# A two-layer hybrid trunk on one core: index scores and later projections interleaved, wide rows counted by ScalarE, experts' second halves one expert later

## The reference

```python
def dsa_mixer(q, k, v, q_idx, k_idx, w_idx, positions, n_sel):   # n_sel = 256
    ...
        rel = jax.nn.relu(jnp.einsum('bqjd,bkd->bqjk', qi_blk, k_idx).astype(F32))   # 8 index heads of 64
        score = jnp.einsum('bqjk,bqj->bqk', rel, wi_blk)
        score = jnp.where((k_pos[None, :] <= q_pos[:, None])[None], score, -jnp.inf)
        _, sel = lax.top_k(score, n_sel)
```

```python
    def expert_block(args):
        xb, e = args
        return (jax.nn.silu(xb @ w_gate[e]) * (xb @ w_up[e])) @ w_down[e]
```

## Time and profile before

| | |
|---|---|
| median of 3 runs | 3084.16 us (3083.2 to 3084.48) |
| the profiled execution | 3082.44 us, of which the span of its instructions is 3080.7 us |
| granted clock of PE, mean | 0.906 of 2.4 GHz |
| PE busy | 2610.5 us (85%) |
| DVE, ACT, POOL busy | 1381.8, 766.0, 375.7 us |
| moved by DMA | 370.42 MB |

### The profile page before, as it was taken

One profiled execution on the slowest core, in us unless ns is written; L12 is line 12 of the kernel. 1 busy time (PEld: TensorE's weight loads), 2 busy tenths in 40 slices (PEclk: granted clock), 3 DMA queues, 4 the chain that ended last, 5 costly groups with the idle time before them and its releaser, 6 DMA issues.

```text
span 3080.7 us, 30243 instructions
## 1 busy us (share of the span) xinstructions
PE 2610.5 (85%) x10356; PEld 1470.3 (48%) x10374; DVE 1381.8 (45%) x3164; ACT 766.0 (25%) x1630; POOL 375.7 (12%) x372
## 2 busy tenths in 40 slices
PE   5979768978999879999579897598889995999994
PEld 2564324545664534444335643245556644444442
DVE  4351498985551321111342516799755414111115
ACT  2121243144450111111112214321545311111112
POOL 0000177100000000000200003750000000000002
PEclk8989958999999889999789897599999997999996
DMA  5100001120000479999311000013010005799974
GB/s 212 39 28 23 28 1 40 41 84 32 11 1 16 165 263 336 333 332 336 144 57 52 1 23 28 0 50 113 2 42 1 10 28 212 285 336 336 335 260 177
DMA packets 105453, 370.42 MB, mean 120 GB/s; under 512 B 20754, under 2 KB 39912, under 8 KB 80744
## 3 DMA queue, kind: packets, MB, share of 16 engines
q1 hardware_dynamic: 91500, 318.41, 29.2%
q0 software_dynamic: 13824, 50.34, 4.3%
HBM read 304.42 MB, written 64.30 MB: 120 GB/s over the span
## 4 chain that ended last, share of the span: by engine, by line
PE 62%; DVE 22%; POOL 5%; issue 5%; ACT 4%; DMA 1%; DVEq 1%; ACTq 0%; SPq 0%; POOLq 0%
PE bank L1017 14%; PE bank L719 9%; PE bank L1034 8%; PE bank L965 7%; DVE group_arena L1671 7%; PE bank L722 6%; PE bank L753 5%; PE bank L683 5%; POOL group_arena L620 4%; PE bank L782 3%; DVE residual L1967 1%; PE bank L1024 1%; PE bank L978 1%; DVE softmax_stats L1512 1%; DVE group_arena L1445 1%
## 5 line engine op out<-in xcount | busy, mean ns | idle before, releaser
L719 PE MATMUL bank<-w_ring,normed_cols 128*128 128x260 f32 (+4 forms) x1280 | 419.0, 490 | 9.8 <-ACTq L1254 8.6
L719 PEld LDWEIGHTS bank<-w_ring,normed_cols 128*128 128x128 f32 x1280 | 245.9, 193 | 183.0 <-issue 158.3
L683 PE MATMUL bank<-ident,group_arena 128*128 128x128 f32 (+1 forms) x1200 | 198.0, 305 | 129.2 <-DVE group_arena L1445 59.8
L722 PE MATMUL bank<-normed_cols,w_ring 128*128 128x512 f32 x640 | 281.5, 601 | 15.5 <-DMA w_ring<-in_w_in 14.3
L640 POOL DMA_INDIRECT group_arena<-h_rows,group_arena x64 | 60.3, 942 | 1631.8 <-DVEq L1927 948.5
L1034 PE MATMUL bank<-heads_cols,group_arena 128*128 128x512 f32 x512 | 236.5, 604 | 7.8 <-DVE group_arena L1937 4.2
L914 PE MATMUL bank<-group_arena 64*128 64x512 f32 (+3 forms) x320 | 159.8, 814 | 95.7 <-ACTq L1254 93.8
L683 PEld LDWEIGHTS bank<-ident,group_arena 128*128 128x128 f32 (+1 forms) x1200 | 148.0, 154 | 189.1 <-issue 94.8
L1017 PE MATMUL bank<-w_ring,group_arena 128*128 128x512 f32 x512 | 230.5, 604 | 1.7 <-issue 1.7
L1017 PE MATMUL bank<-normed_cols,group_arena 128*128 128x512 f32 x512 | 224.9, 592 | 0.0
L965 PE MATMUL bank<-w_ring,heads_cols 128*128 128x512 f32 x512 | 222.6, 594 | 2.0 <-DVEq L250 2.0
(11 more groups left out here) (315 smaller groups left out, 3213.5 us busy)
## 6 DMA issues: line engine op xcount, KB each, us to landing
heads_cols<-in_expert_w_down SPq DMA_DIRECT2D x64, 1024.0 KB, 6.9
w_ring<-in_expert_w_gate SPq DMA_DIRECT2D x32, 1024.0 KB, 5.0
w_ring<-in_expert_w_up SPq DMA_DIRECT2D x32, 1024.0 KB, 7.7
normed_cols<-in_expert_w_gate SPq DMA_DIRECT2D x32, 1024.0 KB, 5.2
normed_cols<-in_expert_w_up SPq DMA_DIRECT2D x32, 1024.0 KB, 7.9
expert_rows<-group_arena SPq DMA_DIRECT2D x64, 512.0 KB, 7.2
w_ring<-in_w_in SPq DMA_DIRECT2D x6, 2048.0 KB, 8.4
expert_rows<-heads_cols SPq DMA_DIRECT2D x1, 8192.0 KB, 29.8
```

What stands on the lines that cost most here:

```text
L683: last = pe.transpose(bank(4 + r % 2)[0:rows, col:col + src.shape[0]], src, ident[0:src.shape[0], 0:src.shape[0]])
L719: m = pe.matmul(proj_bank(n)[:, 0:width], HT[:, k, part * P:(part + 1) * P], w, start=(k == 0), stop=(k == K - 1))
L722: m = pe.matmul(proj_bank(n)[0:width, :], w, HT[:, k, part * HALF:(part + 1) * HALF], start=(k == 0), stop=(k == K - 1))
```

## The change

1. PE now issues the two heads of a pair together, with their halves in turn (`index_pair`, 24 slots), and behind each of the first 16 slots half a group of the later projections (`project_half`, 4 matmuls); so the 8 groups of 420 columns lie between the scores of tiles 7 to 4. The other 16 groups follow the last slot. They use PSUM banks 4 to 7. A pair waits until both relus of the slot before are done; in the slots of tiles 3 and 2 it may be one slot further ahead.
2. Three wide tiles (7, 6 and 5) are counted by ACT's Sign with its accumulator, on the scores themselves: sign(2^24 * (score - candidate)). POOL runs the widest tile's trials as before, but its 1024-column comparison is now a product of one column. DVE runs the trials of tiles 2 to 6 together: it counts 4, 3 and 2, and ACT counts 6 and 5 (`pair_count`). At the end DVE counts the three wide tiles once more exactly, against the next candidate (`wide_end`).
3. ACT runs `pair_count` 31 times, `widest_count` 15 times among them (16 before, in the slots), and the copy of one projection group behind each from the second on.
4. In the experts, PE does gate and up of e, then turns the activation of e-1, turns both halves of the rows of e+1, and does down of e-1. ACT and DVE follow this order. SP's program is not changed there.
5. The load of the latent rows no longer waits for the search; POOL splits the keys between its trials.

```diff
-                for t in reversed(range(2, T)):
-                    for j in range(IDX_HEADS):
...
-                pe.wait_ge(lg_taken, lg.n)
-                project(LATER_CHUNKS)
+                def index_pair(slot):
...
+                    t, pair = SLOTS[slot]
...
+                    free = n if t >= 4 or SLOTS[slot - 1][0] >= 4 else n - 2
+                    if slot >= 1:
+                        pe.wait_ge(lg_taken, free)
+                    at = (slot % 2) * HALF if t < 4 else 0
+                    for c0 in range(0, (t + 1) * P, HALF):
+                        c1 = min(c0 + HALF, (t + 1) * P)
+                        for i in range(2):
+                            m = pe.matmul(PS[i][:, at + c0:at + c1], qTi[i * 64:i * 64 + 64, pair, t * P:(t + 1) * P],
+                                          kTi[i * 64:i * 64 + 64, c0:c1], start=True, stop=True)
+                    m.then_inc(lg_ready, 2)
...
+                for slot in range(len(SLOTS)):
+                    index_pair(slot)
+                    if slot < N_HALVES:
+                        project_half(slot // 2, slot % 2)
+                for group in range(N_HALVES // 2, len(later)):
+                    project_half(group, 0)
+                    project_half(group, 1)
```

ACT, the counts and the order of its work:

```diff
+                def sign_count(t, ready, counted, n):
...
+                    act.wait_ge(ready, n)
+                    act.activation(sign_junk[:, 0:w], flipped[t], ACT.Sign, bias=trial_bias[:, t - 2:t - 1], scale=SIGN_SCALE,
+                                   accum_out=thr[:, 0, t - 2:t - 1]).then_inc(counted, 1)
...
+                def pair_count(n):
+                    for i, t in enumerate(WIDE[1:]):
+                        sign_count(t, pair_trial, pair_counted, n + 1)
+                        act.wait_ge(pair_counted, 2 * n + i + 1)
...
+                for slot in range(len(SLOTS)):
+                    relu_pair(slot)
+                    if slot % 2 == 0 and 2 <= slot <= N_HALVES:
+                        put_later(slot // 2 - 1)
+                    if 4 <= slot < N_HALVES or slot % 2 == 1 and slot > N_HALVES:
+                        widest_count()
+                i = N_HALVES // 2
+                for n in range(31):
+                    pair_count(n)
+                    if n % 2 == 0 and trials.n < 31:
+                        widest_count()
+                    if i < len(later) and n >= 1:
+                        put_later(i)
+                        i += 1
```

DVE, one bit and the end; POOL, the trial; PE, the experts:

```diff
+                def search_bit(b):
...
+                    chain(dve.tensor_scalar(trial_bias[:, wide], thr[:, 4, wide], -SIGN_SCALE, None, ALU.mult))
+                    dve.sem_inc(pair_trial, 1)
+                    counts(NARROW, lambda t: flipped[t], lambda t: thr[:, 4, t - 2:t - 1])
+                    dve.wait_ge(pair_counted, 2 * (31 - b))
+                    take_trial(cols)
...
-                    pool.tensor_scalar(early_mask, flipped[T - 1], cand, None, ALU.is_ge).then_inc(early_masks, 1)
-                    pool.wait_ge(early_counts, 31 - b)
...
+                    pool.tensor_scalar(trial_bias[:, t:t + 1], cand, -SIGN_SCALE, None, ALU.mult).then_inc(trial_ready, 1)
+                    pool.wait_ge(trial_counted, 31 - b)
...
+                        gate_up(e, w, s, q + 1)
+                        finish = not (first and w == 0)
+                        if finish:
+                            turn_a(e - 1, 1 - s)
+                        if not (last and w == NW - 1):
+                            turn_x_lo(e + 1, 1 - s, nx)
+                            turn_x_hi(e + 1, 1 - s)
+                        if finish:
+                            down(e - 1, (w - 1) % NW, 1 - s, q + 1 if w else q)
```

More of the change, by code:

```diff
@@ new lines, in project_half @@
+                def project_half(group, half):
+                    c, use, part, last_use = later[group]
+                    if half == 0:
+                        n = proj.next()
+                        pe.wait_ge(proj_taken, n - 3)
+                        pe.wait_ge(w_loaded[c % 2], 16 * sum(len(CHUNKS[x][0]) for x in range(c % 2, c + 1, 2)))
+                    n = proj.n - 1
+                    kind, _, at, width = use
+                    for k in range(4 * half, 4 * half + 4):
+                        w = WR[:, c % 2, k, at:at + width]
+                        if kind == "row":
+                            m = pe.matmul(later_bank(n)[:, 0:width], HT[:, k, part * P:(part + 1) * P], w,
+                                          start=(k == 0), stop=(k == K - 1))
+                        else:
+                            m = pe.matmul(later_bank(n)[0:width, :], w, HT[:, k, part * HALF:(part + 1) * HALF],
+                                          start=(k == 0), stop=(k == K - 1))
+                    if half == 1:
+                        m.then_inc(proj_ready, 1)
+                        if last_use:
+                            pe.wait_ge(proj_ready, n + 1)
+                            pe.sem_inc(w_used, 1)
@@ L1055, in _ @@
                         turn_x_hi(j + EXPERTS, 0)
-                        expert(j + EXPERTS, 0, 0, j + (QUADS + 1), None, last=True)
+                        gate_up(j + EXPERTS, 0, 0, j + (QUADS + 1))
+                        turn_a(j + EXPERTS, 0)
+                        down(j + EXPERTS, 0, 0, j + (QUADS + 1))
                 barrier(pe, PHASE["experts"])
@@ L1236, in _, with relu_pair @@
                 rel = ATT_DSA[0]
-                i = 0
-                early = Ring()
-                def early_count():
-                    act.wait_ge(early_masks, early.next() + 1)
-                    act.activation(early_mask, early_mask, ACT.Copy, accum_out=thr[:, 0, T - 3:T - 2]).then_inc(early_counts, 1)
-                for t in reversed(range(2, T)):
-                    for j in range(IDX_HEADS):
+                later = list(uses(LATER_CHUNKS))
+                trials = Ring()
+                def relu_pair(slot):
+                    t, _ = SLOTS[slot]
+                    w, at = (t + 1) * P, (slot % 2) * HALF if t < 4 else 0
+                    for i in range(2):
@@ L1377, in _ @@
                         take_x(j + EXPERTS, 0)
-                        expert(j + EXPERTS, 0, last=True)
+                        gate(j + EXPERTS, 0)
                         take_y(j + EXPERTS, 0, j + EXPERTS // 2)
@@ L1691, in search_start, with wide_start @@
                     chain(dve.memset(cur.bitcast(I32), 0))
-                def search_bit(tiles, b):
-                    cols = slice(tiles[0] - 2, tiles[-1] - 1)
-                    count, sign, want, cur, cand, hit = (thr[:, i, cols] for i in range(6))
-                    chain(dve.tensor_tensor(cand.bitcast(I32), cur.bitcast(I32), bits[:, b:b + 1].to_broadcast([P, len(tiles)]), ALU.bitwise_or))
-                    counts(tiles, lambda t: flipped[t], lambda t: thr[:, 4, t - 2:t - 1])
+                def wide_start(t):
+                    search_start(range(t, t + 1))
+                    want = thr[:, 2, t - 2:t - 1]
+                    chain(dve.tensor_copy(real_want[:, t - 2:t - 1], want))
+                    chain(dve.tensor_scalar(want, want, 2.0, float(-1 - (t + 1) * P), ALU.mult, ALU.add))
+                    dve.sem_inc(search_ready, 1)
@@ new lines, in wide_end @@
+                def wide_end():
+                    cols = slice(T - 5, T - 2)
+                    sign, want, cur, cand = (thr[:, i, cols] for i in (1, 2, 3, 4))
+                    dve.wait_ge(search_done, 1)
+                    chain(dve.tensor_copy(want, real_want[:, cols]))
+                    chain(dve.tensor_tensor(cand.bitcast(I32), cur.bitcast(I32), bits[:, 0:1].to_broadcast([P, 3]), ALU.add))
+                    counts(range(T - 3, T), lambda t: flipped[t], lambda t: thr[:, 4, t - 2:t - 1])
+                    take_trial(cols)
+                    chain(dve.scalar_tensor_tensor(cur, cur, float(2.0 ** -126), cur, ALU.is_ge, ALU.mult))
@@ L1719, in _ @@
+                for slot, (t, pair) in enumerate(SLOTS):
+                    for i in range(2):
+                        score(t, 2 * pair + i, 2 * slot + i)
+                    if pair == IDX_HEADS // 2 - 1:
+                        if t in WIDE:
+                            wide_start(t)
+                        elif t == 4:
+                            search_start(range(4, 5))
+                        elif t == 2:
+                            search_start(range(2, 4))
                 for b in range(30, -1, -1):
-                    search_bit(LATE, b)
+                    search_bit(b)
```

198 lines of the change are left out of this document (106 added, 92 removed).

## The result

The changed kernel takes 2939.9 us (median of 4 runs, 2938.8 to 2944.1) against 3083.9 us: ratio 0.954, 95% interval 0.9526 to 0.9554. That is 144 us less; 117 were forecast, and 2939.9 lies inside the range of 2935 to 3018, near its lower end.

The account below looks back on a forecast made before the run. PE was taken as the bound most of the time, with more than a quarter on engines that only search. From 3082.4, 71 us (search) and 46 (experts) are saved: 2965.4 profiled, 2967 us median; range 2935 to 3018.

Parts of the forecast that it names:

- Slots: Search stage, first 16 slots of index pairs with half groups: 5.1 us a slot at tile 7, 79 us in all.
- the change of rows: PE's switch between 64-row and 128-row matmuls in the slots: 0.3 us each, 9.6 us for 32; bounds 0 to 0.8.
- the first part: Search stage's 24 slots up to the joint search, which was to begin 102 us into the stage.
- Rounds 0 to 8: Joint search, early rounds: ACT waits in its copies for PE's 512-column groups, every 6.9 us; 49 us.
- Rounds 9 to 30 and the end: Joint search, later rounds: ACT and DVE in turn, 78 us; then `wide_end`, 5 us.
- the second part: Search stage from the joint search on, 31 bits: 49 + 78 + 5 = 132 us.
- Experts: New order fills PE's idle time between gate/up and down: 0.75 us on 31 experts, 23 us a layer, 46 in two.
- ACT slower: Rival, search stage: ACT becomes the bound, its counts 0.3 us dearer, 17 us a layer less saved; 3001 us; chance 0.17.
- DMA binding: Rival, experts: DMA, already 0.92 busy, binds; gain there near nothing; 3013 us; chance 0.12.
- Low clock: Rival, slots and projections: PE stays at 1.2 GHz, kernel slower than before, up to 3266 us; chance 0.05.
- a slot has no planned wait: Search-stage slots: one reason given against the rival that PE's clock stays low.
- DMA at 0.97 or more: Experts: sign in the next profile that the forecast is right, together with an expert in 11.8 us.

Follow-up runs that it names:

- the experiment with the same partitions: Changed kernel with both heads of each index pair reading partitions 0 to 63, so they can't run side by side; 3001.7 us (ratio 0.9745).
- the third Sign: Changed kernel with a third Sign of 768 columns, result unused, in each round of the joint search; 2981.8 us (ratio 0.9683).
- the kernel without mixing: Changed kernel with PE doing all index pairs first and then all projection groups; 2981.4 us (ratio 0.9678).

## Why the prediction was right, step by step

- **Slots.** Forecast 5.1 us at tile 7 and 79 for 16 slots; measured 4.93, and 74.3 (349.0 to 423.3). The pair at 1.72 is shown by the experiment with the same partitions; the change of rows was 0.14 to 0.2 instead of 0.3. That is most of the difference in the first part: joint search at 97 us into the stage, not 102.
- **Rounds 0 to 8.** Forecast 49 us, bound by PE's groups; measured 446.3 to 495.2, 48.9. The size was right, and so was the wait for this order of instructions. But PE's rate was no bound of the search: in another order of ACT's queue the rounds don't wait for it. The prediction named the wait and what is queued behind it, and put that down as a cost of the change; it was a cost of its order.
- **Rounds 9 to 30 and the end.** Forecast 78 + 5; measured 495.2 to 579.5, 84.3, of which 5.0 are a stall that nobody forecast (below). The rounds themselves were cheaper than forecast by 4 us: two rounds, odd and even, take 3.17 + 3.77 = 6.94 us with copies, where 3.25 + 4.2 were taken, and 3.22 + 3.50 = 6.72 without, where 3.25 + 3.7 were. A copy of 256 columns takes 0.38 us and lengthens two rounds by 0.22. The counts themselves were priced well: with the accumulator's read 1.24, 1.13 and 1.03 us, forecast 1.23, 1.10 and 0.99. That the second part came out at 133.2 us against 132 is luck to this extent: the stall and the cheaper rounds cancel.
- **Experts.** The step that was mis-sized: 0.75 us of idle an expert, 46 in all; measured 1.08 (33.4 us over 31 steps), 68 in all. Ten transposes take 1.12 us, where 1.2 to 1.5 were taken, and down costs 3.48 us behind them, where 3.67 less 0.1 were taken. The forecast fell 27 us short: 22 are here, 6 in the search, and 1 was lost between the stages. The 1.08 us lie above the prediction's own upper bound of 1.0, and 34 us a layer above its 15 to 28; the total stayed inside the range, but just below the 2940 to 2995 that the forecast had for itself. What the new order does was right, and only its size was off.
- **Rivals.** ACT slower: its counts cost what they were priced at, within 0.04 us; ACT does bound 22 rounds, as the third Sign shows. DMA binding: refuted, with 10% more traffic at no cost. Low clock: it didn't come in the slots, and the kernel without mixing shows that it can. The reason given against it, "a slot has no planned wait", was the right one: with a wait of 1.8 to 2.7 us in each slot the clock was 0.63.
- **"DMA at 0.97 or more"** came true (1.00), and says nothing for the forecast: it is 1.01 with 10% more traffic too, at the same time.

## What to carry to other kernels

When a wait on a slow partner stands in an engine's queue ahead of work that is ready, count what stands behind it: eight such copies a layer, moved to every second round, gave 40 us without any work less. Fill a pause of TensorE with work that is due anyway; here it paid twice, in place and in clock. Don't read a DMA share of 1.00 as a limit before more bytes cost time.

## What the hardware showed beside this

One instruction of DVE on 2 columns takes 0.17 us 60 times, and 5.03 us in the last round of each layer. Timeline of the kernel after, of DVE and of POOL:

```profile
563.44 0.17 DVE L1805 TENSOR_SCALAR group_arena<-group_arena 128x2 f32<-128x2 f32 x1
...
565.02 6.92 POOL L646 MEMSET normed_cols<- 2x8192 f32 x1 [0.15 <-POOL group_arena L634]
...
566.34 0.17 DVE L1797 TENSOR_TENSOR group_arena<-group_arena 128x5 int32<-128x5 f32 x1 [0.47 <-ACT group_arena L1318]
...
566.94 5.03 DVE L1805 TENSOR_SCALAR group_arena<-group_arena 128x2 f32<-128x2 f32 x1
```

It ends at 571.97 and POOL's memset at 571.94. In the kernel with the extra Sign it begins later, lasts less, and ends with the memset again (588.88 + 4.05 = 592.93, 585.99 + 6.92 = 592.91):

```profile
585.99 6.92 POOL L646 MEMSET normed_cols<- 2x8192 f32 x1 [0.15 <-POOL group_arena L634]
...
588.88 4.05 DVE L1807 TENSOR_SCALAR group_arena<-group_arena 128x2 f32<-128x2 f32 x1
```

Beside the memset, DVE's tensor_tensor runs at its usual 0.17 us (566.34), and its counts take their usual time. In the kernel before, the memset lay beside the last bits too (from 613.11), where DVE had only such instructions:

```profile
613.11 6.92 POOL L633 MEMSET normed_cols<- 2x8192 f32 x1 [63.95 <-ACT heads_cols L1271]
...
617.27 0.88 DVE L1671 TENSOR_SCALAR_CACHE_REDUCE group_arena<-group_arena 128x640 bf16<-128x640 f32 x1
```

The new fp32 `tensor_scalar` for ACT's bias (the second instruction of `search_bit`) is what made it a stall. The Trainium skill (SBUF — State Buffer, "SBUF: two separate sides") says that DVE in a two-port mode and GpSimd take a shared port pair for a whole instruction, and block each other; the trace agrees, with one long instance in each layer of all twelve kernels here that have the new search, 5.02 to 5.04 us, and 4.05 to 4.06 in the one with the extra Sign. The ends of the two instructions agree within some 0.03 us each time. In which mode DVE's instruction ran, no row shows. The memset was not moved, so that the 10 us (two layers) which its move could give are argued and not shown.
